# Order of work at four of TensorE's waits: last down block, convolution's way out, expert places, state-space norm

## The chip, the cores and the metric

One core of one Trainium2 chip runs the whole program in one launch. The metric is the device time of an execution in microseconds; shorter is better. All arithmetic is on float32 data. Most matrix products split both operands into a high part (rounded to the matmul's own fp32r format) and a low part (the rest), and add three products: high by high, high by low, low by high.

## The reference, cut to what matters

Two blocks follow each other on a sequence of 256 tokens with 1024 features. The first has two layers, the second two more:

```python
for layer in range(2):                      # first_block
    x = x + 0.5 * rmsnorm(swiglu(rmsnorm(x), gate, up, down))
    hdn = nsa_ssd_mixer(rmsnorm(x), ...) if layer == 0 else rwkv7_time_mix(rmsnorm(x), ...)
    x = x + rmsnorm(hdn)
    x = x + 0.5 * rmsnorm(swiglu(rmsnorm(x), gate, up, down))
for i in range(2):                          # second_block
    mod = silu(c) @ ada_w[i] + ada_b[i]     # shift, scale, gate, shift, scale, gate
    h = rmsnorm(x) * (1 + sc1) + sh1
    y = short_conv_mixer(h) if i == 0 else gated_deltanet_mixer(h)
    x = x + gt1 * rmsnorm(y)
    h = rmsnorm(x) * (1 + sc2) + sh2
    x = x + gt2 * rmsnorm(hier_moe(h))      # 64 experts, each token goes to two; one shared expert
```

The short convolution mixer is `W_out(B * conv3(C * (W x)))`. The mixer with attention and state space puts 512 features of attention and 1024 of the state-space part side by side, the latter gated and normalized in two groups, and multiplies the 1536 by one output matrix. `swiglu` has 2816 hidden features.

## The kernel before, in words

The program is a list of ten stages: Ffn, NsaSsd, Ffn, Ffn, Rwkv, Ffn, Conv, Moe, Delta, Moe. Every engine has its own instruction stream, written out by hand stage by stage in methods `pe`, `act`, `dve`, `pool` and in `sync_program`, and an engine runs its stream strictly in order. The order between engines is kept by named signals: `up` raises one with an instruction, `ge` is waited for. Nothing is planned at run time, so the place of a line in these methods is the order of work.

Weights come in slots of 1 MB. SyncE issues one transfer for each slot, in the order of use, into a ring of six places (more in some stages). A place is free when its last reader has signalled, and SyncE waits for that in order, too. Of a slot, half (128 x 1024) is a unit: ScalarE copies it to the high part (`split_act`, L764, in `Ffn` L922 and L937), VectorE subtracts to get the low part (`split_dve`, L770, in `Ffn` L929 and L943), and TensorE multiplies (`mm3`, L811 to L813). The split parts lie in a buffer of three units, so the split of unit u waits until TensorE has done unit u-3. The data operand is split in the same way in pieces of 128 features, called chunks below: `source_hi` and `source_act` on ScalarE (L783, L793), `source_lo` and `source_dve` on VectorE (L801). Output products (`out_rows_pe`) go through the chunks, and each takes four groups of three matmuls of 512 columns, one group for each of the PSUM banks 0 to 3.

The end of every stage (`back_act`, `back_dve`) squares and sums the four banks on ScalarE as they are done (`y_done`, L694), bank by bank; for each half of the tokens (two banks) it forms the inverse deviation (L697, L710), and VectorE scales (L716) and adds to `x` (L723). The next stage begins with transposes of `x`, which wait for this.

The four places that the change touches:

- **Ffn, last block.** A block b of 256 hidden features has gate and up products, SiLU and product (L976, L1019), a transpose of the result (`turn_pe`, L1085), its split (high part on ScalarE, L981; low part on VectorE, L1025) and the down product (`down_pe`), which adds 24 matmuls to banks 0 to 3. In other blocks the next block's gate and up products lie between the transpose and the down product; behind the last block (b = 10) there is nothing. `down_pe` waits for the low part of the hidden features before its first matmul. VectorE's order in block 10 is: low part of the down weights' second half (L943), then low part of the hidden features (L1025). The last block's loop has the bank outside, so that a bank is done after 6, 12, 18 and 24 matmuls.
- **Conv, way out.** Units 0 to 23 are the input products, two each of the parts B, C and x for four groups of 256 features; units 24 to 31 are the output product. VectorE (L1193 to L1200) and GpSimd (L1220) make the convolution's output chunk by chunk beside the input products. All eight chunks are split after unit 23, since they go into the buffer `x_r`, which the input products read; the splits of units 24 and 25 stand behind them in both queues. TensorE has only the spread of the gain (L678) to do meanwhile.
- **Moe, places.** `select_dve(0)` (L1512, L1514: four operations) makes the matrices by which the tokens of the first four experts are gathered (`gather_pe`, L1527). It stands behind `shared_dve(3)`, which waits for the shared expert's last product.
- **NsaSsd, way out.** The attention's four chunks of `mix` are ready before the state-space part begins. That part ends with the gating (L3133), squares (L3097), sums (`sums_pe`, L603), deviation (L609), reciprocal (L614) and scaling (L3138) of two groups of four chunks. Between the gating and the norm VectorE has a step of the modulation (`fill`, L2025) that waits for TensorE's products of the modulation (L1997, L2007). TensorE's fill of group 8 stands ahead of the output product in its queue; ScalarE then copies that group's row (L2016), which the output product waits for, as banks 2 and 3 hold the modulation. Then ScalarE and VectorE split all 12 chunks, and only then unit `out0 + 2`.

The piece of code that orders the way out of NsaSsd in TensorE's stream is

```python
        self.ssd_pe(e)
        self.x_r = self.x_r_out
        e.wait_ge(*k.ge("attention_out", n, TT - 1))
        e.wait_ge(*k.ge("mod_row", 8))
        e.wait_ge(*k.ge("mod_added", 7))
        self.out_rows_pe(e, self.out0, "mix", 12)
```

## Time and profile before

| | |
|---|---|
| time, median of 3 runs | 3057.51 us (3055.89 to 3057.93) |
| the profiled execution's own time | 3057.37 us |
| its span in the profile | 3055.5 us |
| TensorE busy | 2815.4 us (92%) |
| VectorE, ScalarE, GpSimd busy | 1293.3, 1122.6, 161.4 us |
| mean granted clock of TensorE | 0.958 |
| read from HBM | 697.50 MB |

The span is the time from the first to the last recorded instruction; the execution's own time is 1.9 us longer. A busy share is an average over ten stages with different limits, so it tells where to look and not what an edit is worth. The clock is a share of 2.4 GHz: TensorE is granted either all of it or half (1.2 GHz). Rows name an engine, a line of the kernel and the tensors that are written and read; a value in brackets is the engine's idle time ahead of the instruction, and what ended it.

### The profile page before, as it was taken

What the parts mean: (1) busy time and instruction counts of PE and PEld (TensorE: products, weight loads), DVE (VectorE), ACT (ScalarE), POOL (GpSimd) and SP (SyncE); (2) the same over time, 40 slices, a digit from 0 to 9 for tenths busy, and PEclk for the clock granted to TensorE, in tenths of its full rate; (3) what the DMA queues carried; (4) which work ended last, traced back from release to release, by engine and by line L of the source; (5) the groups of instructions that cost most, each with busy time, mean ns of one, the idle gap of its engine ahead of it and who ended that gap; (6) DMA issues with size and microseconds to landing.
All of it is one profiled execution on the core that took longest, in us unless ns stands there. A gap on an engine that the chain in (4) does not pass through costs nothing.

```text
span 3055.5 us, 44024 instructions
## 1 busy us (share of the span) xinstructions
PE 2815.4 (92%) x18364; PEld 2218.1 (73%) x18364; DVE 1293.3 (42%) x2125; ACT 1122.6 (37%) x2008; POOL 161.4 (5%) x146
## 2 busy tenths in 40 slices
PE   8989878999989998799899999999896879999998
PEld 7879657887878888578697666666695856666665
DVE  5556266546557543464454121212484542221212
ACT  5444245435447222254443222222454251222222
POOL 0000000000000222100010000000002400000000
PEclk9989899999989999799999999999897989999999
DMA  8424656436424111065244899999550036999996
GB/s 338 188 97 165 265 239 268 180 137 234 180 111 193 43 56 56 28 229 195 101 165 159 351 415 415 416 414 417 230 185 1 1 124 255 417 415 418 415 417 252
DMA packets 96402, 701.55 MB, mean 230 GB/s; under 512 B 10688, under 2 KB 10816, under 8 KB 11328
## 3 DMA queue, kind: packets, MB, share of 16 engines
q1 hardware_dynamic: 96192, 698.59, 57.6%
q8 instruction: 151, 2.47, 0.3%
q14 instruction: 59, 0.48, 0.0%
HBM read 697.50 MB, written 1.05 MB: 229 GB/s over the span
## 4 chain that ended last, share of the span: by engine, by line
PE 86%; DVE 6%; ACT 4%; issue 2%; DMA 1%; POOL 1%; SPq 0%; DVEq 0%; ACTq 0%
PE bank L1549 14%; PE bank L811 12%; PE bank L813 12%; PE bank L812 12%; PE bank L1609 8%; PE bank L1527 4%; PE bank L1636 4%; PE bank L1887 2%; PE bank L1895 2%; PE bank L1899 2%; DMA weight_ring<-weight_slots 1%; DVE h_sb L716 1%; PE bank L2402 1%; PE bank L1418 1%; PE bank L1421 1%
## 5 line engine op out<-in xcount | busy, mean ns | idle before, releaser
L1549 PE MATMUL bank<-weight_ring,packed_h 128*64 128x256 f32 x2176 | 285.4, 379 | 0.0
L811 PE MATMUL bank<-source_hi_lo,weight_hi_lo 128*128 128x256 f32 x864 | 250.4, 290 | 13.7 <-DVE source_hi_lo L801 11.7
L1549 PE MATMUL bank<-more_slots,packed_h 128*64 128x256 f32 x1920 | 257.0, 379 | 1.5 <-ACT packed_h L1536 1.5
L811 PE MATMUL bank<-gate_up_hi_lo,x_hi_lo 128*128 128x512 f32 x640 | 253.2, 396 | 1.3 <-DVE gate_up_hi_lo L929 1.3
L1549 PEld LDWEIGHTS bank<-weight_ring,packed_h 128*64 128x64 f32 x2176 | 196.6, 137 | 74.0 <-issue 18.1
L813 PE MATMUL bank<-gate_up_hi_lo,x_hi_lo 128*128 128x512 f32 x640 | 249.7, 390 | 0.0
L812 PE MATMUL bank<-gate_up_hi_lo,x_hi_lo 128*128 128x512 f32 x640 | 249.1, 389 | 0.0
L812 PE MATMUL bank<-source_hi_lo,weight_hi_lo 128*128 128x256 f32 x864 | 247.9, 287 | 0.0
L813 PE MATMUL bank<-source_hi_lo,weight_hi_lo 128*128 128x256 f32 x864 | 247.7, 287 | 0.0
L1549 PEld LDWEIGHTS bank<-more_slots,packed_h 128*64 128x64 f32 x1920 | 174.2, 137 | 69.4 <-issue 15.4
L770 DVE TENSOR_TENSOR weight_hi_lo<-weight_ring,weight_hi_lo 128x1024 fp32r<-128x1024 f32 x138 | 168.0, 1221 | 106.3 <-ACT weight_hi_lo L764 106.2
L1565 DVE TENSOR_TENSOR packed_hidden<-packed_silu,bank 128x256 f32<-128x256 f32 x64 | 27.0, 421 | 415.5 <-ACT packed_silu L1558 415.5
L1626 DVE SCALAR_TENSOR_TENSOR expert_out_hi_lo<-bank,place_gates,expert_out_hi_lo 128x512 fp32r<-128x512 f32 x128 | 96.1, 751 | 223.7 <-ACT expert_out_hi_lo L1620 223.7
L811 PEld LDWEIGHTS bank<-source_hi_lo,weight_hi_lo 128*128 128x128 f32 x864 | 169.4, 196 | 16.7 <-issue 16.1
L943 DVE TENSOR_TENSOR down_hi_lo<-weight_ring,down_hi_lo 128x1024 fp32r<-128x1024 f32 x72 | 87.8, 1224 | 205.5 <-ACT down_hi_lo L937 205.5
L764 ACT ACTIVATE weight_hi_lo<-weight_ring 128x1024 fp32r<-128x1024 f32 x144 | 151.3, 1054 | 61.4 <-PE bank L813 56.8
L1558 ACT ACTIVATE packed_silu<-bank 128x256 f32<-128x256 f32 x64 | 24.6, 384 | 403.9 <-PE bank L1549 403.9
L812 PEld LDWEIGHTS bank<-source_hi_lo,weight_hi_lo 128*128 128x128 f32 x864 | 169.5, 196 | 0.2
L813 PEld LDWEIGHTS bank<-source_hi_lo,weight_hi_lo 128*128 128x128 f32 x864 | 169.4, 196 | 0.0
L937 ACT ACTIVATE down_hi_lo<-weight_ring 128x1024 fp32r<-128x1024 f32 x72 | 75.9, 1059 | 222.0 <-PE bank L813 222.0
L929 DVE TENSOR_TENSOR gate_up_hi_lo<-weight_ring,gate_up_hi_lo 128x1024 fp32r<-128x1024 f32 x128 | 151.5, 1219 | 11.5 <-ACT gate_up_hi_lo L922 11.5
L1609 PE MATMUL bank<-weight_ring,hidden_T 128*64 128x512 f32 x544 | 146.0, 597 | 10.4 <-issue 10.4
(540 smaller groups left out, 5446.7 us busy)
## 6 DMA issues: line engine op xcount, KB each, us to landing
weight_ring<-weight_slots SPq DMA_DIRECT2D x443, 1024.0 KB, 7.6
more_slots<-weight_slots SPq DMA_DIRECT2D x212, 1024.0 KB, 9.0
params_sb<-small_params SPq DMA_DIRECT2D x1, 3196.5 KB, 17.6
h_sb<-weight_slots SPq DMA_DIRECT2D x3, 1024.0 KB, 5.6
y_sb<-weight_slots SPq DMA_DIRECT2D x3, 1024.0 KB, 7.7
x_sb<-x_by_tokens SPq DMA_DIRECT2D x1, 1024.0 KB, 4.9
out_by_tokens<-x_sb SPq DMA_DIRECT2D x4, 256.0 KB, 2.2
params_sb<-small_params SPq DMA_DIRECT2D x1, 69.5 KB, 4.6
```

Of the source, the lines that this page charges most:

```text
L764: e.activation(self.shaped(w[:, 0, :], src), src, ACT.Copy).then_inc(*k.up("weights_hi", self.n, u))
L770: e.tensor_tensor(self.shaped(w[:, 1, :], src), src, self.shaped(w[:, 0, :], src).bitcast(F32), ALU.subtract).then_inc(*k.up(*self.lo_key(u)))
L811: e.matmul(out, w[0], x[0], start=start, stop=False, skip_group_check=shared)
L812: e.matmul(out, w[0], x[1], start=False, stop=False, skip_group_check=shared)
L813: return e.matmul(out, w[1], x[0], start=False, stop=stop, skip_group_check=shared)
L929: e.tensor_tensor(lo, src, hi.bitcast(F32), ALU.subtract).then_inc(*k.up(*self.lo_key("gate_up", j, m)))
L943: e.tensor_tensor(lo, src, hi.bitcast(F32), ALU.subtract).then_inc(*k.up(*self.lo_key("down", b, fc)))
L1527: mm = e.matmul(ps[:, j * T:(j + 1) * T], self.h_tok[:, part, q, c * P:(c + 1) * P], self.sel[g % 2][:, q, :, :].rearrange("p e s -> p (e ...
L1549: mm = e.matmul(ps[x * CAP:(x + 1) * CAP, m * FB:(m + 1) * FB], self.hc[:, c, (2 * (p % 2) + x) * CAP:(2 * (p % 2) + x + 1) * CAP], wt[:, ...
L1609: mm = e.matmul(ps[x * CAP:(x + 1) * CAP, :], self.turned[p % 2][:, fc * P + x * CAP:fc * P + (x + 1) * CAP], wd[:, fc * D + m * 512:fc * ...
L1626: e.scalar_tensor_tensor(out=self.out[p % 2][:, 1, cut], in0=k.banks.at(n, "down", p, m)[:, :], scalar=self.slot_gate[:, p % 2:p % 2 + 1], ...
L1636: mm = e.matmul(k.bank[b][:, :], self.scatter[p % 2][:, b // 2 * P:b // 2 * P + P], self.out[p % 2][:, part, b % 2 * 512:b % 2 * 512 + 512 ...
```

## The change

In `Ffn`, the last block's down product gets a method of its own, `last_down_pe`. It begins with the eight matmuls that need only the high part of the first 128 hidden features, when `hidden_hi` is there, and then does the other sixteen, four for each bank. VectorE makes the low part of the hidden features first and the down weights' low part second. In `Conv`, the chunks of the output get a buffer of their own, `out_hi_lo`; chunks 0 to 5 are split beside the input products (two each at units 8, 14 and 20), and the splits of units 24 and 25 move into the loop. In `Moe`, `select_dve(0)` moves ahead of `shared_dve(3)`. In `NsaSsd`, the attention's four chunks are split during the state-space part, VectorE's step of the modulation moves between the norm's first and second group, and unit `out0 + 2` and the remaining splits alternate with the chunks. No matmul, no transfer and no byte is added or removed.

```diff
@@ -1019,11 +1019,13 @@
                 e.scalar_tensor_tensor(out=self.hid[:, q, :], in0=k.banks.at(n, "gate_up", b, q)[:, FB:2 * FB], scalar=k.x_inv[:, q:q + 1], in1=self.silu[:, q, :],
                                        op0=ALU.mult, op1=ALU.mult).then_inc(*k.up("hidden", n, b, q))
             before, behind = self.around_turn(b)
-            for split in before:
-                self.split_dve(e, split)
+            last = b == FFN_BLOCKS - 1
+            if not last:
+                for split in before:
+                    self.split_dve(e, split)
             e.wait_ge(*k.ge("hidden_hi", n, b))
             e.tensor_tensor(self.hid_r[:, 1, :, :], halves(k.banks.at(n, "hidden_T", b)), self.hid_r[:, 0, :, :].bitcast(F32), ALU.subtract).then_inc(*k.up("hidden_lo", n, b))
-            for split in behind:
+            for split in before if last else behind:
                 self.split_dve(e, split)
         self.back_dve(e, lambda f: self.gain_in(), 0.5)
 
@@ -1087,22 +1089,36 @@
 
     def down_pe(self, e, b):
         k, n = self.k, self.n
-        last = b == FFN_BLOCKS - 1
-        e.wait_ge(*k.ge("hidden_lo", n, b))
 
         def part(bank, fc):
             x, cut = self.hid_r[:, :, fc, bank // 2 * P:bank // 2 * P + P], slice(bank % 2 * 512, bank % 2 * 512 + 512)
-            return self.mm3(e, k.bank[bank][:, :], (x[:, 0, :], x[:, 1, :]), (self.d_r[:, fc, 0, cut], self.d_r[:, fc, 1, cut]), b == 0 and fc == 0, last and fc == 1)
+            return self.mm3(e, k.bank[bank][:, :], (x[:, 0, :], x[:, 1, :]), (self.d_r[:, fc, 0, cut], self.d_r[:, fc, 1, cut]), b == 0 and fc == 0, False)
+        e.wait_ge(*k.ge("hidden_lo", n, b))
         for fc in range(2):
             e.wait_ge(*k.ge(*self.lo_key("down", b, fc)))
-            if not last:
-                for bank in range(4):
-                    mm = part(bank, fc)
-                mm.then_inc(*k.up("down", n, b, fc))
-        if last:
             for bank in range(4):
-                part(bank, 0)
-                part(bank, 1).then_inc(*k.up("y_done", n, bank))
+                mm = part(bank, fc)
+            mm.then_inc(*k.up("down", n, b, fc))
+
+    def last_down_pe(self, e):
+
+        k, n, b = self.k, self.n, FFN_BLOCKS - 1
+
+        def one(bank, fc, part, w_part, stop=False):
+            x, cut = self.hid_r[:, part, fc, bank // 2 * P:bank // 2 * P + P], slice(bank % 2 * 512, bank % 2 * 512 + 512)
+            return e.matmul(k.bank[bank][:, :], x, self.d_r[:, fc, w_part, cut], start=False, stop=stop)
+        e.wait_ge(*k.ge("hidden_hi", n, b))
+        e.wait_ge(*k.ge(*self.lo_key("down", b, 0)))
+        for bank in range(4):
+            one(bank, 0, 0, 0)
+            one(bank, 0, 0, 1)
+        e.wait_ge(*k.ge("hidden_lo", n, b))
+        e.wait_ge(*k.ge(*self.lo_key("down", b, 1)))
+        for bank in range(4):
+            one(bank, 0, 1, 0)
+            one(bank, 1, 0, 0)
+            one(bank, 1, 1, 0)
+            one(bank, 1, 0, 1, True).then_inc(*k.up("y_done", n, bank))
 
     def pe(self, e):
         k, n = self.k, self.n
@@ -1119,7 +1135,7 @@
                 self.gate_up_pe(e, b + 1, 1)
                 if b + 2 < FFN_BLOCKS:
                     self.down_pe(e, b)
-        self.down_pe(e, FFN_BLOCKS - 1)
+        self.last_down_pe(e)
 
 
 class Conv(Stage):
@@ -1133,28 +1149,38 @@
         self.out, self.taps = self.sb("conv_out", [P, C, T]), self.sb("conv_taps", [P, 2, T])
         self.units = []
         self.product_buffers(self.mem)
+        self.x_r_in, self.x_r_out = self.x_r, self.sb("out_hi_lo", [P, 2, C, T], F32R)
         self.plan_units(12, column_half, 2)
         self.plan_units(4, row_half)
 
+    def done_at(self, u):
+
+        return (u // 3 - 2, u // 3 - 1) if u % 6 == 2 and u > 6 else ()
+
     def pe(self, e):
         k, n = self.k, self.n
         self.begin(e)
         self.norm_pe(e)
+        self.x_r = self.x_r_in
         for u in range(24):
             part = u % 6 // 2
             empty = (("conv_b", n, u), ("conv_gate", n, u), ("conv_u", n, u))[part]
             ps = k.banks.take(e, (n, "unit", u), empty)
             self.columns_pe(e, u, ps[:, 0:T], "h" if u == 0 else None)
         self.spread_pe(e, k.gain[:, 0, 1, :])
+        self.x_r = self.x_r_out
         self.out_rows_pe(e, 24, "out")
 
     def act(self, e):
         k, n = self.k, self.n
         e.wait_ge(*k.ge("modulation", 0))
+        self.x_r = self.x_r_in
         self.norm_act(e, k.gain[:, 0, 0, :], k.mod[0][:, 0:C], lambda c: self.source_hi(e, "h", k.h, c, self.h_key(c)), lambda: self.split_act(e, 1))
+        self.x_r = self.x_r_out
         for u in range(24):
-            if u + 2 < 24:
-                self.split_act(e, u + 2)
+            self.split_act(e, u + 2)
+            for c in self.done_at(u):
+                self.source_hi(e, "out", self.out, c, ("conv_out", n, c))
             part, m = u % 6 // 2, u % 2
             c = 2 * (u // 6) + m
             ps = k.banks.at(n, "unit", u)[:, 0:T]
@@ -1167,9 +1193,8 @@
                 e.wait_ge(*k.ge("unit", n, u))
                 e.activation(self.g_T[:, m, :], ps, ACT.Copy).then_inc(*k.up("conv_gate", n, u))
         self.spread_act(e)
-        self.source_act(e, "out", self.out, [("conv_out", n, c) for c in range(C)], ("unit", n, 23))
-        self.split_act(e, 24)
-        self.split_act(e, 25)
+        for c in (6, 7):
+            self.source_hi(e, "out", self.out, c, ("conv_out", n, c))
         for u in range(24, 30):
             self.split_act(e, u + 2)
         self.back_act(e)
@@ -1177,10 +1202,13 @@
     def dve(self, e):
         k, n, K = self.k, self.n, self.TAPS
         e.wait_ge(*k.ge("modulation", 0))
+        self.x_r = self.x_r_in
         self.norm_dve(e, k.gain[:, 0, 0, :], k.mod[0][:, 0:C], lambda c: self.source_lo(e, "h", k.h, c))
+        self.x_r = self.x_r_out
         for u in range(24):
-            if u + 2 < 24:
-                self.split_dve(e, u + 2)
+            self.split_dve(e, u + 2)
+            for c in self.done_at(u):
+                self.source_lo(e, "out", self.out, c)
             part, m = u % 6 // 2, u % 2
             c = 2 * (u // 6) + m
             if part == 2:
@@ -1199,9 +1227,8 @@
                     e.wait_ge(*k.ge("conv_taps", n, c, t - 1))
                     e.scalar_tensor_tensor(out=taps, in0=self.u_T[:, c, t:t + T], scalar=w(t), in1=taps,
                                            op0=ALU.mult, op1=ALU.add).then_inc(*k.up("conv_taps", n, c, t))
-        self.source_dve(e, "out", self.out)
-        self.split_dve(e, 24)
-        self.split_dve(e, 25)
+        for c in (6, 7):
+            self.source_lo(e, "out", self.out, c)
         for u in range(24, 30):
             self.split_dve(e, u + 2)
         self.back_dve(e, lambda f: k.ge("gain_row", n, f))
@@ -1681,7 +1708,6 @@
         return over
 
     def experts_dve(self, e):
-        self.select_dve(e, 0)
         for p in range(self.PAIRS):
             if p == self.PAIRS - 1:
                 over = self.overflow_load(e)
@@ -1833,6 +1859,7 @@
         for u in range(3):
             self.shared_dve(e, u)
         self.ranks_dve(e)
+        self.select_dve(e, 0)
         self.shared_dve(e, 3)
         over = self.experts_dve(e)
         self.overflow_dve(e, over)
@@ -3091,6 +3118,8 @@
         for x, step in self.four_steps():
             k.modulation.fill(e, "ACT", int(step == 2 and x >= 4))
             self.four_act(e, x, step)
+            if step == 2 and x >= 4:
+                self.source_hi(e, "mix", self.mix, x - 4, ("attention_out", n, TT - 1))
         self.sqrt_table(e)
         for c in range(C):
             e.wait_ge(*k.ge("ssd_gated", n, c))
@@ -3131,8 +3160,11 @@
         e.wait_ge(*k.ge("ssd_y", n, 7, 1))
         for c in range(C):
             e.tensor_tensor(self.mix[:, 4 + c, :], self.mix[:, 4 + c, :], self.silu_z[:, c, :], ALU.mult).then_inc(*k.up("ssd_gated", n, c))
-        k.modulation.fill(e, "DVE", 4)
         for g in range(2):
+            for c in (2 * g, 2 * g + 1):
+                self.source_lo(e, "mix", self.mix, c)
+            if g:
+                k.modulation.fill(e, "DVE", 4)
             self.inverse_dve(e, f"ssd{g}", k.rms[:, g, :])
             for c in range(4 * g, 4 * g + 4):
                 e.scalar_tensor_tensor(out=self.mix[:, 4 + c, :], in0=self.mix[:, 4 + c, :], scalar=k.par("ssd_norm")[:, c:c + 1], in1=k.rms[:, g, :],
@@ -3169,11 +3201,15 @@
         e.wait_ge(*k.ge("attended", n, TT - 1, 3))
         self.split_act(e, self.out0)
         self.split_act(e, self.out0 + 1)
+        self.x_r = self.x_r_out
         self.ssd_act(e)
-        self.x_r = self.x_r_out
-        self.source_act(e, "mix", self.mix, [("ssd_out", n, C - 1)] + [None] * 11)
-        for u in range(self.out0, self.out0 + 10):
-            self.split_act(e, u + 2)
+        self.split_act(e, self.out0 + 2)
+        for c in range(C):
+            self.source_hi(e, "mix", self.mix, 4 + c, ("ssd_out", n, c))
+            if c % 2 and c < 6:
+                self.split_act(e, self.out0 + 3 + c // 2)
+        for u in range(self.out0 + 6, self.out0 + 12):
+            self.split_act(e, u)
         self.back_act(e)
 
     def dve(self, e):
@@ -3184,11 +3220,15 @@
         self.attention_dve(e)
         self.split_dve(e, self.out0)
         self.split_dve(e, self.out0 + 1)
+        self.x_r = self.x_r_out
         self.ssd_dve(e)
-        self.x_r = self.x_r_out
-        self.source_dve(e, "mix", self.mix, 12)
-        for u in range(self.out0, self.out0 + 10):
-            self.split_dve(e, u + 2)
+        self.split_dve(e, self.out0 + 2)
+        for c in range(C):
+            self.source_lo(e, "mix", self.mix, 4 + c)
+            if c % 2 and c < 6:
+                self.split_dve(e, self.out0 + 3 + c // 2)
+        for u in range(self.out0 + 6, self.out0 + 12):
+            self.split_dve(e, u)
         self.back_dve(e, lambda f: self.gain_in())
 
     def early_pool(self, e):
```

## Rows read from the trace of the kernel before

**Rows 1.** The page, part 4: shares of the chain that ended last, by engine.

```profile
PE 86%; DVE 6%; ACT 4%; issue 2%; DMA 1%; POOL 1%; SPq 0%; DVEq 0%; ACTq 0%
```

**Rows 2.** TensorE's waits: line, who released it, us in total, times, longest us.

```profile
PE bank L811 <- DVE hidden_hi_lo L1025: 8.4, 4, 2.1
...
PE bank L811 <- DVE weight_hi_lo L770: 7.1, 4, 5.3
...
PE bank L1527 <- issue: 1.6, 2, 0.8
```

**Rows 3.** Timeline of TensorE, last down blocks of Ffn 0 and Ffn 2.

```profile
199.87 0.80 PE L811 MATMUL bank<-down_hi_lo,hidden_hi_lo 128*128 128x512 f32 x1 [2.09 <-DVE hidden_hi_lo L1025]
...
688.20 0.80 PE L811 MATMUL bank<-down_hi_lo,hidden_hi_lo 128*128 128x512 f32 x1 [2.09 <-DVE hidden_hi_lo L1025]
```

**Rows 4.** Timeline of ScalarE, last blocks of Ffn 0 and Ffn 2.

```profile
197.86 0.58 ACT L981 ACTIVATE hidden_hi_lo<-bank 128x512 fp32r<-128x512 f32 x1
...
204.33 0.60 ACT L694 ACTIVATE h_sb<-bank 128x512 f32<-128x512 f32 x1 [0.81 <-PE bank L813]
...
693.72 0.60 ACT L694 ACTIVATE h_sb<-bank 128x512 f32<-128x512 f32 x1 [1.87 <-PE bank L813]
```

**Rows 5.** Timeline of VectorE, last block of Ffn 0.

```profile
197.99 1.22 DVE L943 TENSOR_TENSOR down_hi_lo<-weight_ring,down_hi_lo 128x1024 fp32r<-128x1024 f32 x1 [0.70 <-ACT down_hi_lo L937]
199.13 0.68 DVE L1025 TENSOR_TENSOR hidden_hi_lo<-bank,hidden_hi_lo 128x512 fp32r<-128x512 f32 x1
...
208.11 0.15 DVE L708 TENSOR_SCALAR out_part<-y_square_sums 128x1 f32<-128x1 f32 x1
```

**Rows 6.** Windows: us, busy us of the five engines, granted clock, DMA share, GB/s.

```profile
450.00:452.00 2.00, 0.53 (x3) 0.51 (x4) 1.97 (x7) 1.09 (x5) 0.00 (x0) 1.00 1.00 422
469.30:497.00 27.70, 27.70 (x124) 22.94 (x123) 11.70 (x10) 10.21 (x12) 0.00 (x0) 1.00 0.57 204
1604.98:1609.30 4.32, 4.32 (x10) 3.42 (x11) 2.22 (x2) 0.59 (x1) 0.00 (x0) 0.51 0.42 159
```

**Rows 7.** Timeline of TensorE, way out of Conv.

```profile
1597.70 1.95 PE L678 MATMUL bank<-params_sb,mod_gain 128*128 128x128 f32 x16
1604.98 0.79 PE L811 MATMUL bank<-weight_hi_lo,source_hi_lo 128*128 128x512 f32 x1 [5.34 <-DVE weight_hi_lo L770]
```

**Rows 8.** Timeline of ScalarE, VectorE and GpSimd, Conv.

```profile
1602.63 2.94 ACT L764 ACTIVATE weight_hi_lo<-weight_ring 128x1024 fp32r<-128x1024 f32 x3
...
1582.44 1.22 DVE L770 TENSOR_TENSOR weight_hi_lo<-weight_ring,weight_hi_lo 128x1024 fp32r<-128x1024 f32 x1
1584.88 1.23 DVE L770 TENSOR_TENSOR weight_hi_lo<-weight_ring,weight_hi_lo 128x1024 fp32r<-128x1024 f32 x1 [1.22 <-ACT weight_hi_lo L764]
...
1582.61 1.66 POOL L1220 TENSOR_TENSOR conv_out<-conv_taps,conv_b 128x256 f32<-128x256 f32 x1 [1.27 <-DVE conv_taps L1200]
...
1599.83 0.72 POOL L1220 TENSOR_TENSOR conv_out<-conv_taps,conv_b 128x256 f32<-128x256 f32 x1 [2.14 <-DVE conv_taps L1200]
```

**Rows 9.** Timeline of VectorE, last shared product of Moe 0.

```profile
1678.09 0.42 DVE L1446 TENSOR_TENSOR hid<-silu,bank 128x256 f32<-128x256 f32 x1 [6.70 <-ACT silu L1440]
```

**Rows 10.** The chain in order of time, NsaSsd: start us, us, what.

```profile
448.41 6.85 DMA weight_ring<-weight_slots
```

**Rows 11.** Groups of ScalarE, NsaSsd 410:465: count, busy, mean ns, idle before.

```profile
L3048 ACT ACTIVATE seg_T<-seg_T 128x512 f32<-128x512 f32 x8 | 5.0, 626 | 7.8 <-DVE seg_T L3063 7.8
```

**Rows 12.** Timeline of TensorE, ScalarE, VectorE, way out of NsaSsd.

```profile
456.94 2.80 PE L1997 MATMUL bank<-weight_ring,silu_c 128*32 128x256 f32 x48
465.00 0.77 PE L811 MATMUL bank<-weight_hi_lo,source_hi_lo 128*128 128x512 f32 x1 [5.27 <-DVE source_hi_lo L801]
...
459.86 0.38 ACT L2016 ACTIVATE mod_rows<-bank 128x256 f32<-128x256 f32 x1 [4.18 <-PE bank L1997]
...
457.13 1.74 DVE L614 RECIPROCAL inv_rms<-inv_rms 128x256 f32<-128x256 f32 x1
...
464.43 4.11 DVE L801 TENSOR_TENSOR source_hi_lo<-mix_in,source_hi_lo 128x256 fp32r<-128x256 f32 x12 [0.48 <-ACT source_hi_lo L793]
```

## The prediction

> **What bounds the kernel now.** I read the page first: 86% of the chain that ended last lies on TensorE [rows 1], so an edit is worth what it takes from TensorE's waits, or from the stretches between stages in which TensorE waits for the sums. Next I read TensorE's waits by releaser [rows 2]. The reader is to find in it 8.4 us in four waits for the low part of the hidden features (one in each Ffn), 5.3 us in one wait for weights (Conv; the other three of that row are short), and 1.6 us in two waits ahead of the gather, which the trace puts down to nobody. The fourth place is a wait of 5.3 us for source chunks [rows 12]. Together that is 20.6 us of idle time. The timelines of each place then show what stands in the queue ahead of the releaser [rows 3 to 5, 7 to 9, 12], and windows show the granted clock around them [rows 6]: behind a long wait the matmuls run at the lower level of 1.2 GHz (a mean of 0.51 in Conv) for some four microseconds. So a removed wait can pay twice.
>
> Two speeds recur. At the full clock, 124 matmuls of 512 columns take 27.70 us, 0.223 us each; the first ten in Conv, at a mean clock of 0.51, take 4.32 us, 0.43 us each [rows 6]. Ten matmuls at the full clock would take 2.2 us: a spell of low clock costs 2.1 us.
>
> The sum is made against the profiled execution's own time of 3057.37 us, 0.14 us below the median of the three runs; I subtract from the median at the end.
>
> **Ffn, last block, four times.** The number of matmuls stays at 24. Before, the high part of the hidden features ends at 197.86 + 0.58 = 198.44 [rows 4]; VectorE is at that time in the down weights' low part (197.99, 1.22 us), makes the low part of the hidden features from 199.13 to 199.81, and TensorE begins at 199.87 after 2.09 us of idle time [rows 3, 5]. After, TensorE can begin 0.06 us behind the high part, at 198.5. Its eight matmuls last until 200.3. VectorE takes 0.6 us for the hidden features (the distance to the next instruction is a little less than its length) and 1.22 us for the weights, and is done at 200.3, so that the other sixteen begin at 200.4. The added wait on the second half's low part stands here, and costs under 0.1 us. Behind VectorE's swapped pair nothing is queued but the stage's end.
>
> What counts is not the last bank but the second one: the token half's scaling on VectorE starts with it, and the second half's first operation stands behind it in the queue (208.11 [rows 5]). The second bank is now done with matmul 16, not 12: 200.4 + 8 x 0.223 + 0.3 (its own length, and the longer first one) = 202.5. Before, its square begins at 204.33 [rows 4]. The gain is 1.9 us: the earlier start gives 1.4, the seven or so matmuls that are no longer slow give 7 x 0.21 = 1.4, and four more matmuls ahead of the second bank take 0.9 back. In Ffn 2 the same stretch, first matmul to second square, takes 693.72 - 688.20 = 5.5 us and not 4.5 [rows 3, 4], since the low clock lasts longer; there the gain is 2.9 us. I take 1.9 for the other two: 1.9 + 2.9 + 1.9 + 1.9 = 8.6 us. This holds if the clock stays up. TensorE's wait shrinks from 2.09 to 0.7 us; a wait of 1.7 us in NsaSsd leaves the clock at 1.00, though TensorE is busy for only 0.53 of 2 us [rows 6]. Bounds for one block: at the full clock 1.9 (2.9); at the low level for all sixteen, 16 x 0.43 = 6.9, it would be 1.3 us slower than now; with one spell of 2.1 us, about zero.
>
> **Conv, way out.** Before, the spread of the gain ends at 1597.70 + 1.95 = 1599.65, and TensorE waits 5.34 us for unit 24's low part [rows 7]. In the change units 24 and 25 and chunks 0 to 5 are ready by then: unit 24 may be split once unit 21 is done. So the wait goes whole, 5.3 us, and with it the spell of low clock, 2.1 us: 7.4 us. Late next is unit 26, which needs ScalarE's gain copies and chunks 6 and 7 before it. TensorE needs it after two chunks, 24 x 0.223 = 5.4 us behind 1599.7, at 1605.1. GpSimd's last product ends at 1599.83 + 0.72 = 1600.6 [rows 8]; ScalarE's chunk 0.4 and unit 1.0 (2.94 for three [rows 8]) and VectorE's 1.2 make 1603.3: 1.8 us to spare. The six chunks split in the loop add 0.7 us to VectorE and 0.8 us to ScalarE at three units; VectorE idles 1.22 us ahead of such a unit's split [rows 8], ScalarE still more, since it waits for TensorE there. Without that cover they would cost 0.8 us at each of the three, 2.4 us. The transfers of later slots start earlier with their splits, in the same order.
>
> GpSimd's product of 128x256 took 1.66 us at 1582.61, when VectorE ran the weight split of 1582.44, and 0.72 us at 1599.83, when it ran none [rows 8]. The splits keep their 1.22 us. The Trainium skill, SBUF — State Buffer, section "Who interferes with whom", says that VectorE and GpSimd share one pair of ports under an exclusive lock, and the loser waits; by that, the moved splits could delay chunks 6 and 7. By that rule, with the last two products stretched by 0.9 us each, the part would still be 7.4 us, with nothing to spare; one more such delay would make it 6.5 us. The trace agrees with the rule.
>
> **Moe, places, twice.** VectorE idles 6.70 us ahead of `shared_dve(3)`; the four operations on 128x256, at 0.42 us like the one of the row 1.7 us, fit there [rows 9]. `shared_dve(3)` is not delayed, as they are done before its input is there. TensorE's two waits ahead of the gather go, 1.6 us in both stages together [rows 2]; uncovered, the moved operations could give nothing and cost 1.7 us a stage.
>
> **NsaSsd, way out.** Before, TensorE's last fill product ends at 456.94 + 2.80 = 459.74, and the output product begins at 465.00, after 5.27 us of idle time [rows 12]. After, it waits only for ScalarE's row of group 8, 459.86 + 0.38 = 460.24 [rows 12], and begins at 460.3: 4.7 us. The wait left is 0.6 us, so the low clock goes as well, 2.1 us: 6.8 us. The floor under this is a transfer: group 8's weights land at 448.41 + 6.85 = 455.26 [rows 10] and hold the fill; the change doesn't touch it. Late next is unit `out0 + 2`: the norm's first group began at 457.13, behind the modulation's sum, and ended with the second at 463.9 [rows 12]; freed of that it can begin some 3 us earlier, with four chunks of 0.34 us (4.11 us for twelve) put in. It ends near 461.7, the unit's low part near 463, and TensorE needs it at 460.3 + 5.4 = 465.7. The four chunks that ScalarE copies within the state-space part, 0.4 us each, lie in its idle time, of which 7.8 us stand ahead of the eight operations of L3048 alone [rows 11]; uncovered they would be 1.6 us.
>
> **Sum.** 8.6 + 7.4 + 1.6 + 6.8 = 24.4 us. 3057.5 - 24.4 = 3033.1 us.
>
> **Rivals.** *The clock falls in the last block all the same* (10%). For it: there are two short pauses around the transposes. Against: the 1.7 us wait without a fall. The 8.6 us go, 15.8 stay: 3041.7 us. *A second wait behind the removed one* (7%): unit 26 in Conv or `out0 + 2` in NsaSsd is late, as VectorE has to finish chunks before the split in both. It would take 2 to 3 us each; with half of both starts lost, 5 us: 3038 us. For it: one in-order queue; against: margins of 1.8 and 2.7 us. *The edits do not move the ends* (4%): the next stage is held by transfers that don't start earlier. The DMA share is 0.57 in the NsaSsd product [rows 6], so it would have to be in every stage: 3057 us. *Slower* (3%): the low clock stays through the products that now start without a pause, in Conv and NsaSsd, 96 + 144 matmuls. Each costs 0.21 us more; from 24.4 / 0.21 = 116 such matmuls on the change loses. All 240 would cost 50 us less the 20.2 us of waits gone: 3087 us. Against it: no product in the windows stays low for more than a spell.
>
> **Numbers.** The forecast has 76%. Its own bounds: up to 26.4 us if all Ffn ends give 2.9, with the runs' spread of 1.6 us 3029.5; upwards to the first rival. I take 3029.5 to 3041.8, which leaves out under 2 in 10. About 0.2%, 6 us, can be told from no change by a measurement of this kernel. Faster: 76 + 10 + 7 = 93%; same 4%; slower 3%.
>
> **What would show it.** TensorE's wait on hidden features near 0.7 us and its second square 1.9 us earlier to the start of the block; no wait of L811 on weights in Conv, and L811 behind L678 at the full clock; a wait of 0.6 us on ScalarE's row ahead of the NsaSsd product; no wait ahead of the first gather. A granted clock at the lower level at any of the first three would prove that step wrong, and so would a new wait on L770 at chunk 2.

## Result and profile after

The changed kernel takes 3036.2 us (median of 4 runs, 3035.5 to 3036.9), the kernel before 3057.7 (4 runs, 3055.9 to 3062.0) beside it: a ratio of 0.9928, with a 95% interval of 0.9912 to 0.9944. That is 21.5 us less; 24.4 us had been forecast, 3033.1 us, and the measured time lies within the range. The profiled execution took 3035.50 us over a span of 3033.6 us, 21.9 us below the span of before. What is left to explain is the 2.9 us by which the gain falls short.

The chain of the changed kernel by engine, against [rows 1], has not moved:

```profile
PE 86%; DVE 6%; ACT 4%; issue 2%; DMA 1%; POOL 1%; SPq 0%; DVEq 0%; ACTq 0%
```

TensorE's waits in the changed kernel (line, releaser, total us, times, longest us), against [rows 2]:

```profile
PE bank L1109 <- ACT hidden_hi_lo L981: 2.9, 4, 0.7
PE bank L811 <- DVE weight_hi_lo L770: 2.8, 5, 1.3
```

Four waits of 2.09 us are now four of 0.71 us, on ScalarE. The wait of 5.34 us in Conv is gone. What is left in the row of L770 stands in the Rwkv stage: the 1.3 us (at 962.75) and two of 0.24 us stood there before, two of 0.56 and 0.40 us (at 903.06 and 921.13) are new. The two waits ahead of the gather are not listed any more.

**Ffn 0, last block.** Timelines of TensorE, VectorE and ScalarE, changed kernel, against [rows 3 to 5]:

```profile
198.44 5.83 PE L1109 MATMUL bank<-down_hi_lo,hidden_hi_lo 128*128 128x512 f32 x24 [0.71 <-ACT hidden_hi_lo L981]
...
198.42 0.69 DVE L1027 TENSOR_TENSOR hidden_hi_lo<-bank,hidden_hi_lo 128x512 fp32r<-128x512 f32 x1 [1.19 <-ACT hidden_hi_lo L981]
199.03 1.22 DVE L943 TENSOR_TENSOR down_hi_lo<-weight_ring,down_hi_lo 128x1024 fp32r<-128x1024 f32 x1
...
202.49 0.60 ACT L694 ACTIVATE h_sb<-bank 128x512 f32<-128x512 f32 x1 [0.22 <-PE bank L1109]
...
206.27 0.15 DVE L708 TENSOR_SCALAR out_part<-y_square_sums 128x1 f32<-128x1 f32 x1
```

TensorE starts at 198.44 and does all 24 matmuls without a pause, VectorE is done at 200.25, and the second square comes at 202.49 where it came at 204.33; the second half's first operation follows at 206.27, not 208.11. The start, VectorE's end and the second square were forecast to 0.1 us.

**NsaSsd and Conv, ways out.** Timelines of the changed kernel, NsaSsd first (TensorE, ScalarE, VectorE, then for Conv TensorE, VectorE and GpSimd), against [rows 12] and [rows 7, 8]:

```profile
462.96 0.47 PE L811 MATMUL bank<-weight_hi_lo,source_hi_lo 128*128 128x512 f32 x1 [0.61 <-issue]
...
462.48 0.38 ACT L2043 ACTIVATE mod_rows<-bank 128x256 f32<-128x256 f32 x1 [4.17 <-PE bank L2024]
...
464.20 1.22 DVE L770 TENSOR_TENSOR weight_hi_lo<-weight_ring,weight_hi_lo 128x1024 fp32r<-128x1024 f32 x1
...
1586.11 1.95 PE L678 MATMUL bank<-params_sb,mod_gain 128*128 128x128 f32 x16
1587.81 0.47 PE L811 MATMUL bank<-weight_hi_lo,out_hi_lo 128*128 128x512 f32 x1
...
1590.46 1.23 DVE L770 TENSOR_TENSOR weight_hi_lo<-weight_ring,weight_hi_lo 128x1024 fp32r<-128x1024 f32 x1 [0.53 <-ACT weight_hi_lo L764]
...
1585.37 1.64 POOL L1247 TENSOR_TENSOR conv_out<-conv_taps,conv_b 128x256 f32<-128x256 f32 x1 [12.70 <-DVE conv_taps L1228]
1588.29 0.74 POOL L1247 TENSOR_TENSOR conv_out<-conv_taps,conv_b 128x256 f32<-128x256 f32 x1 [1.28 <-DVE conv_taps L1228]
```

In NsaSsd 0.61 us of the 5.27 us are left, and the first matmul takes 0.47 us and not 0.77. The trace names no releaser for this wait; ScalarE's row ends at 462.86, 0.1 us ahead of the product. In Conv the product follows the spread without a pause; unit 26 is ready at 1591.7 where TensorE reaches it at 1593.4, 1.7 us to spare. Of GpSimd's last two products the first is stretched: 1.64 us beside VectorE's weight split of 1585.21, where it took 0.73 us in the kernel before. The last one takes 0.74 us, with VectorE idle from 1588.2 to 1589.0. So of the two delays that the prediction allowed by the rule of the Trainium skill (SBUF — State Buffer, "Who interferes with whom") one occurs, and it costs nothing: TensorE has no wait in the product.

**Moe, places.** Timelines of TensorE around the first gather, before and after:

```profile
1677.47 1.95 PE L678 MATMUL bank<-params_sb,mod_gain 128*128 128x128 f32 x16
1680.20 1.07 PE L1527 MATMUL bank<-places,h_tokens_hi_lo 128*128 128x256 f32 x7 [0.78 <-issue]
```
```profile
1659.19 1.95 PE L678 MATMUL bank<-params_sb,mod_gain 128*128 128x128 f32 x16
1660.89 1.19 PE L1554 MATMUL bank<-places,h_tokens_hi_lo 128*128 128x256 f32 x8
```

The gather began 2.73 us behind the start of the spread and now begins 1.70 us behind it: 1.03 us for a wait of 0.78 us. The rest is overlap. Where nothing is waited for, a matmul starts 0.25 us before the recorded end of the one ahead of it, and the idle time does not count that.

**Stretch by stretch.** Windows cut at the same events in each kernel show more than the totals: from the last hidden features of an Ffn to the next stage's first transposes (an "end"), from NsaSsd's start to its last fill product, from there to the output product, and so on. Columns: stretch, us, TensorE busy us (matmuls), granted clock, DMA share, GB/s. The kernel before, first profile; in this order: end of Ffn 0, NsaSsd to its last fill product, to the output product, to the next stage, ends of Ffn 2 and 3, Rwkv, Conv's start (to its first product C * x), Conv's way out:

```profile
196.41:211.26 14.85, 8.30 (x30) 0.83 0.20 71
211.26:456.94 245.68, 212.59 (x2091) 0.91 0.55 215
456.94:465.00 8.06, 2.79 (x49) 0.83 0.83 321
465.00:500.55 35.55, 34.83 (x145) 0.94 0.60 225
...
684.74:697.12 12.38, 9.74 (x30) 0.72 0.24 86
...
881.80:896.83 15.03, 8.49 (x31) 0.85 0.19 70
896.83:1318.94 422.11, 378.64 (x2800) 0.93 0.22 83
...
1518.35:1543.19 24.84, 20.26 (x138) 0.75 0.42 154
...
1597.70:1633.26 35.56, 25.98 (x115) 0.90 0.41 151
```

The same nine stretches of the changed kernel:

```profile
196.36:209.41 13.05, 6.96 (x30) 1.00 0.23 82
209.41:459.55 250.14, 216.64 (x2090) 0.89 0.54 211
459.55:462.96 3.41, 2.80 (x50) 1.00 0.78 327
462.96:496.56 33.60, 32.89 (x144) 1.00 0.74 281
...
680.87:690.40 9.53, 6.95 (x31) 1.00 0.31 110
...
874.93:887.99 13.06, 6.97 (x30) 0.90 0.22 80
887.99:1308.42 420.43, 375.76 (x2800) 0.94 0.22 83
...
1505.94:1531.59 25.65, 21.08 (x138) 0.72 0.41 149
...
1586.11:1614.10 27.99, 23.75 (x115) 0.97 0.53 191
```

The edited places gain 1.8 + 2.85 + 2.0 + 1.9 us (Ffn; the last from 14.99 to 13.05), 4.65 + 1.95 (NsaSsd), 7.6 (Conv) and 1.0 twice (Moe, from the router's product to the first hidden features of the experts, 60.04 to 59.01): 24.8 us between these two profiles. The stretches that the diff does not touch take 2.9 us back: NsaSsd up to the fill 4.5, Conv's start 0.8, the first Moe's start 0.9 (9.58 to 10.46), less 1.7 in Rwkv and 1.4 in Delta (308.40 to 306.98), the others 0.1 less. So in this pair of profiles the missing 2.9 us lie where nothing was changed. The experiments ask why, and whether the parts are what the sum took them for.

### The profile page after: what moved, and what is told of

Same layout as the page of the kernel before. It is cut to its first block, busy times and chain, and to the rows that moved or that the text cites. A ratio compares the mean times of both kernels' runs of the same rounds, so it can differ in the third digit from the quotient of the medians.

```text
span 3033.6 us, 44027 instructions
## 1 busy us (share of the span) xinstructions
PE 2805.1 (92%) x18364; PEld 2211.1 (73%) x18364; DVE 1293.2 (43%) x2125; ACT 1121.9 (37%) x2008; POOL 162.3 (5%) x146
## 4 chain that ended last, share of the span: by engine, by line
PE 86%; DVE 6%; ACT 4%; issue 2%; DMA 1%; POOL 1%; SPq 0%; DVEq 0%; ACTq 0%
PE bank L1576 15%; PE bank L811 11%; PE bank L813 11%; PE bank L812 11%; PE bank L1636 8%; PE bank L1554 4%; PE bank L1663 4%; PE bank L1914 2%; PE bank L1922 2%; PE bank L1926 2%; DMA weight_ring<-weight_slots 1%; DVE h_sb L716 1%; PE bank L2429 1%; PE bank L1445 1%; PE bank L1448 1%
## 5 line engine op out<-in xcount | busy, mean ns | idle before, releaser
L770 DVE TENSOR_TENSOR weight_hi_lo<-weight_ring,weight_hi_lo 128x1024 fp32r<-128x1024 f32 x138 | 168.2, 1221 | 100.6 <-ACT weight_hi_lo L764 100.6
```

The source lines that it names most:

```text
L770: e.tensor_tensor(self.shaped(w[:, 1, :], src), src, self.shaped(w[:, 0, :], src).bitcast(F32), ALU.subtract).then_inc(*k.up(*self.lo_key(u)))
```

## Experiments

Medians go with the runs of the kernel before on the same chip. The local times, read from each profile as above, follow the verdicts in one table.

**One part at a time.** Each kernel is the kernel before with one part of the diff, word for word: the last block of the Ffn stages, Conv, Moe, NsaSsd.

> The kernel before with the last block of the four Ffn stages as in the change, and nothing else. Theory (the whole change fell short of the sum because the earlier end of Ffn 0 is taken back in NsaSsd, where TensorE's granted clock falls in other places; the code there is untouched): the four ends still gain 1.85 + 2.75 + 1.9 + 1.8 = 8.3 us by the trace of the changed kernel, NsaSsd takes some 4.3 us back, net about 4 us: 3053.5 us, 0.9987 of before, with a stretch of low clock of over 3 us near 281 and one longer than before from 325. Rival (the parts are worth what the prediction said, and the shortfall comes from the NsaSsd part or from an interplay): 8.3 to 8.6 us faster, 3049 us, 0.9972, the clock between 280 and 345 as before.

> The kernel before with Conv's way out as in the change, and nothing else. All theories: 7.4 us (the wait of 5.3 us and the low clock behind it) less up to 1.3 us for a new short wait of the output product on a weight split, 0.9 us more if the stage behind it gives some back: 3049.5 to 3051.5 us, 0.9974 to 0.9980. It is here as a part of the sum: if NsaSsd, which comes earlier, is unmoved, the clock between 280 and 345 stays as before.

> The kernel before with the places of the first pair made ahead of the shared expert's last quarter in both Moe stages, and nothing else. Prediction's term: 1.6 us, 3056.1 us, 0.9995. By the trace of the changed kernel 1.0 us in the first Moe stage and 1.3 us in the second lie around it, 2.3 us, 0.9992. Rival (nothing on the path): 1.000.

> The kernel before with NsaSsd's way out as in the change, and nothing else. Theory (the part itself works and the loss in NsaSsd comes from the earlier start, which this kernel does not have): 6.3 to 6.8 us faster, 3051 us, 0.9978 to 0.9979, and between 210 and 440 no event moves by more than 0.3 us. Rival (the part causes the loss of 4.3 us ahead of its own place): 2 to 2.5 us faster, 3055 us, 0.9992, with the low clock near 281.

Against 3061.2 us before: Ffn alone 3050.2 us, 0.9964 (0.9951 to 0.9978); Conv alone 3047.1, 0.9957 (0.9944 to 0.9971); Moe alone 3052.2, 0.9974 (0.9963 to 0.9985); NsaSsd alone 3054.4, 0.9971 (0.9959 to 0.9983). Ffn gained 11.0 us by the medians, Conv 14.1, Moe 9.0 and NsaSsd 6.8. NsaSsd alone is what was expected of it; the others gained more than any expectation allowed. The medians add up to 41 us, twice the whole. In the places themselves the parts gain about what was forecast (the table below). The fourth kernel fells the theory on NsaSsd: its Ffn 0 ends as before, yet NsaSsd up to the last fill product takes 7.4 us longer than in the first profile of before:

```profile
211.46:464.56 253.10, 219.18 (x2091) 0.88 0.54 208
```

The low clock near 281 that the Ffn kernel was to show is there (280.4 to 283.8), but so it is in this one (282.5 to 285.9). It could still come from these two parts themselves, so the kernel before and the changed one were run again as they are.

**The same two kernels once more, and the change without its Ffn part.** The third kernel is the changed one with the last block's order of the kernel before.

> The kernel before, unchanged, a second time with a profile. The four kernels with one part each moved by up to 8 us in stretches of NsaSsd (280 to 460) that their code leaves as it was. Theory (the places of TensorE's low clock differ from execution to execution of one and the same program, and carry several us): this profile differs from the first one of the kernel before by 3 us or more at some point of NsaSsd, and the granted clock between 280 and 460 is at the lower level in other places. Rival (the clock follows from the program alone, and each edit moves it): the two profiles agree within 0.5 us everywhere.

> The changed kernel, unchanged, a second time with a profile. Theory (the sum of 24.4 us is right place by place, and the shortfall of some 3 us is the clock in untouched stretches): in this profile the gains between two events on either side of each edited place are again 1.8, 2.7, 1.9, 1.8 (Ffn), 7.5 (Conv), 1 to 1.3 twice (Moe) and 6.4 us (NsaSsd) within 0.4 us, while the whole difference to a profile of before on this chip is anywhere from 18 to 30 us. Rival (NsaSsd always takes 4.3 us back when Ffn 0 ends earlier): the loss of 4 us or more between 210 and 345 against before is there again.

> The changed kernel with the last block of the four Ffn stages as before. Theory (the parts add up, and the clock in untouched stretches only adds spread): 8.4 us slower than the changed kernel on the same chip, within 3 us, some 0.9948 of before. Rival (the earlier end of Ffn 0 costs 4.3 us in NsaSsd each time, which this kernel is spared): 4 us slower than the changed kernel or less, 0.9935 or less of before.

Before 3057.9 us (17 runs, 3052.8 to 3065.4), a second set of the same program 3057.9 (12 runs); changed 3036.9 (6 runs, 3032.8 to 3039.3), 0.9926 (0.9911 to 0.9941): the result again, 20.9 us. Without Ffn 3041.2, 0.9938 (0.9923 to 0.9954): 4.3 us, between the two expectations, and the interval holds both. The second profile of the kernel before, stretches from NsaSsd's start to the fill product and the ends of Ffn 2 and Ffn 3:

```profile
211.49:461.74 250.25, 217.33 (x2090) 0.89 0.54 211
...
689.65:700.88 11.23, 8.20 (x30) 0.85 0.27 95
...
884.71:898.13 13.42, 6.86 (x30) 0.97 0.20 78
```

One program, two executions: NsaSsd differs by 4.6 us at a clock of 0.91 and 0.89 (from 282.9 to 286.3 the second is granted 0.50, the first 1.00), the end of Ffn 3 by 1.6 us at 0.85 and 0.97, with the same wait in it. TensorE's first matmul behind that wait, in the first and in the second profile:

```profile
885.25 0.55 PE L811 MATMUL bank<-down_hi_lo,hidden_hi_lo 128*128 128x512 f32 x1 [2.09 <-DVE hidden_hi_lo L1025]
...
888.16 0.50 PE L811 MATMUL bank<-down_hi_lo,hidden_hi_lo 128*128 128x512 f32 x1 [2.09 <-DVE hidden_hi_lo L1025]
```

In the first the clock falls at 885.6, while the products run; in the second it stays up until 897.3, when they are done. So a wait of this length is followed by low clock in some executions and not in others. The chip is not the reason: 17 executions of the kernel before on one chip took 3052.8 to 3065.4 us, the fastest at a mean granted clock of 0.960, the slowest at 0.954. The Trainium skill (TensorE: Matmul & The Clock Gate, Part 1) says that the phase of the chip's activity monitor runs freely, so that one kernel meets different numbers of slow matmuls from run to run. The page says it of a kernel's start; these profiles show the same in the middle of one. The rival of a fixed loss from Ffn 0's earlier end falls too: without the Ffn part the stretch takes 250.28 us, with it 250.14 and 249.90.

**Three edits of the changed kernel, to test single terms.**

```diff
# e7: last block of Ffn, order of the matmuls
-        for bank in range(4):
+        for bank in range(3):
             one(bank, 0, 0, 0)
             one(bank, 0, 0, 1)
+            if bank < 2:
+                one(bank, 1, 0, 0)
...
# e8: Conv's chunks all behind the loop (the same on ScalarE)
-            for c in self.done_at(u):
-                self.source_lo(e, "out", self.out, c)
...
-        for c in (6, 7):
+        for c in range(C):
             self.source_lo(e, "out", self.out, c)
# e9: NsaSsd, VectorE
+        k.modulation.fill(e, "DVE", 4)
         for g in range(2):
             for c in (2 * g, 2 * g + 1):
                 self.source_lo(e, "mix", self.mix, c)
-            if g:
-                k.modulation.fill(e, "DVE", 4)
```

> The changed kernel with another order in the last block of the Ffn stages: ahead of the wait for the low parts, banks 0 and 1 get three of their six matmuls and bank 2 two, in place of two for each of the four banks; so the second bank is done with matmul 14 and not 16. Theory (the second bank's square sets the end of the stage): from the last hidden features to the next stage's first transposes 12.6 us and not 13.05, 0.45 us (two matmuls) in each of the four ends, 1.8 us in all, too little for the median to show. Rival (the last bank sets it): 13.05 us as before in all four.

> The changed kernel with all eight chunks of Conv's output split after the loop, and only the splits of units 24 and 25 left in it. It tells what the buffer with its early chunks is worth beside the moved weight splits. Theory (after the spread of the gain only chunk 0 is late: ScalarE's copy behind its gain copies, 0.4 us, and VectorE's 0.35 us behind it): TensorE waits 1.4 us for chunk 0 and for nothing else, the clock stays up, and the way out takes 29.4 us from the spread to the next stage and not 27.99. Rival one (the low clock comes with this wait too): 31.5 us. Rival two (unit 26 is late behind eight chunks as well): over 30 us with a second wait on a weight split at the third unit.

> The changed kernel with VectorE's modulation sum ahead of the state-space norm again, as in the kernel before. Theory (the norm then starts 3.1 us later, and the low part of the third unit of the output product, ready at 465.4 in the changed kernel where TensorE reaches it at 468.4, comes 3.8 us later): a wait of 0.8 us at the third unit, and 34.4 us from the product's start to the next stage and not 33.6; the product itself starts as in the changed kernel. Rival (the sum's place is worth the whole wait of before): 3 us or more. Rival two (the margin holds): 33.6 us.

Medians: 3031.6, 3035.1 and 3035.9 us against 3057.9 before, each with an interval of some 6 us either way, which tells none of them from the changed kernel. The stretches tell all three. e7: all four ends take 0.45 us less, as expected. The first, and ScalarE's second square in it:

```profile
197.33:209.93 12.60, 6.96 (x30) 0.95 0.22 84
```
```profile
203.01 0.60 ACT L694 ACTIVATE h_sb<-bank 128x512 f32<-128x512 f32 x1
```

That is 5.05 us behind the turn's first transpose at 197.96, where the changed kernel has 202.49 - 196.99 = 5.50. The second bank sets the end, as the prediction had it. (Conv's start behind the last end takes 25.84 us and not 25.65 to 25.70, which gives part of one of the four back.) e8: TensorE waits once, for a chunk, and the matmul behind it is at the full clock:

```profile
1589.08 0.47 PE L811 MATMUL bank<-weight_hi_lo,out_hi_lo 128*128 128x512 f32 x1 [1.54 <-DVE out_hi_lo L801]
```

The way out takes 29.74 us (29.4 expected), against 27.99 with the early chunks and 35.5 before. So within the way out the moved weight splits are worth 5.8 us and the buffer with its chunks 1.75. The next stage takes part of the buffer's share back: the first Moe's start takes 10.46 us in the changed kernel and 9.60 in e8, so that 0.9 us are left. e9: the product starts as in the changed kernel, 3.40 us behind the fill product, and the third unit is late:

```profile
471.59 0.51 PE L811 MATMUL bank<-weight_hi_lo,source_hi_lo 128*128 128x512 f32 x1 [0.42 <-DVE weight_hi_lo L770]
```

The wait is 0.42 us, not 0.8, but with the overlap of some 0.2 us that it also breaks and a slower matmul behind it the cost is what was expected: from the start of the product to the next stage it is 34.40 us. Of the 6.6 us of this part the sum's place is worth 0.8.

**Work for TensorE while it waits.** In the changed kernel six stages begin with matmuls at the low clock, behind a wait of 4.2 to 7.7 us. The diff is the longer version; the shorter one has 18, 5 and 10 for 34, 8 and 16.

```diff
         for q in range(TT):
+            if q and busy:
+                self.keep_busy(e, busy)
...
     def norm_pe(self, e):
...
+        self.keep_busy(e, 34)
-        self.turn_in_pe(e, self.k.h_tok, lambda q, f: (("scaled_second" if f else "scaled_first", n, q),), lambda c: (self.h_key(c, 0),))
+        self.turn_in_pe(e, self.k.h_tok, lambda q, f: (("scaled_second" if f else "scaled_first", n, q),), lambda c: (self.h_key(c, 0),), 8)
+        self.keep_busy(e, 16)
+
+    def keep_busy(self, e, count):
+        for signal in k.banks.until.get(5, ()):
+            e.wait_ge(*k.ge(*signal))
+        for _ in range(count):
+            e.matmul(k.bank[5][:, 0:P], k.par("ident"), k.par("ident"), start=True, stop=True)
```

> The changed kernel, with extra matmuls of 128 columns on the identity into a free bank where TensorE waits at the start of the six stages that begin with the scaled input (34 ahead of the first transposes, 8 ahead of the second eight, 16 ahead of the first product). Their results are not used. Theory (a wait lets the clock fall, and the low clock behind it is paid by what follows): the clock stays at the full level through these starts; the transposes of the second token half take 1.2 to 1.7 us and not 1.97, and the first product's 3.9 us at the low level take 2 us less; 2 to 3 us for each of six stages, 12 to 18 us faster than the changed kernel, 0.988 of before. Rival (the extra matmuls only bring the low clock elsewhere, or end later than the waits they stand in): the same time or up to 6 us slower.

> The kernel with extra matmuls again, but fewer: 18 ahead of the first transposes, 5 ahead of the second eight, 10 ahead of the first product. In the longer version one extra matmul took 0.225 us at the full clock, so that 34 took 7.65 us in a wait of 5.1 us and each stage began 2.6 us late (15.67 us and not 13.05 for the ends of Ffn); that ate what the clock gave. Theory: 18 fit into the wait (4.05 us of 4.2 to 5.1 us), the ends of Ffn take 13.05 us again, the starts stay at the full clock as in the longer version (Conv's start 21.3 us or less and not 25.7, Rwkv 3 us shorter), and the kernel is 13 to 18 us faster than the changed kernel: 3021 us, 0.988 of before. Rival (in the last microsecond of the wait, which is now empty, the clock falls all the same): the changed kernel's time within 2 us.

The longer one 3039.4 us, 0.9933 (0.9918 to 0.9947); the shorter one 3033.8, 0.9917 (0.9903 to 0.9930). Neither can be told from the changed kernel, where 12 to 18 us had been expected of each. Timeline of TensorE in the shorter one, the end of the last Ffn (extra matmuls, L638) and Conv's start, then its windows for Rwkv, Conv's start and the first Moe's start:

```profile
1504.28 4.29 PE L638 MATMUL bank<-params_sb 128*128 128x128 f32 x36
1509.37 1.07 PE L552 MATMUL bank<-params_sb,y_sb 128*128 128x128 f32 x8 [0.81 <-ACT y_sb L576]
...
1517.84 0.36 PE L822 MATMUL bank<-source_hi_lo,weight_hi_lo 128*128 128x256 f32 x1 [1.81 <-DVE source_hi_lo L812]
```
```profile
891.13:1311.89 420.76, 376.44 (x2831) 0.95 0.22 83
...
1509.37:1532.51 23.14, 20.17 (x168) 1.00 0.47 164
1615.02:1625.24 10.22, 9.00 (x64) 1.00 0.97 407
```

The clock does stay up where TensorE is kept busy: 1.00 in Conv's start, where the changed kernel has 0.72. But the gain is 2.5 us there (25.65 to 23.14), nothing in Rwkv (420.76 us, against 420.43 and 421.03 in the two profiles of the changed kernel) and 0.2 in the first Moe's start (10.46 to 10.22). The second Moe's start takes 10.22 us where the changed kernel has 9.54: its extra matmuls end later than the wait they stand in, and push the first product back. In Conv's start the first product stands at 8.47 us behind the first transposes with or without extra work (25.70 us in the changed kernel's second profile, its first product at 1515.44), since it waits for VectorE's chunk: faster transposes buy nothing, only the product after it. So a low clock costs its full price only where TensorE itself sets the pace. The longer version has 417.70 us in Rwkv, but an end of Ffn 3 of 15.67 us ahead of it, together no less than the changed kernel's 13.06 + 420.43. Why Rwkv gives nothing at 0.95 against 0.94 is open.

Local times by profile, in us. "Ffn ends" are those of Ffn 0, 2, 3 and 5, "Moe places" is the first of the two:

| kernel | median | Ffn ends | NsaSsd to fill | fill to next stage | Conv's start | way out | Moe places |
|---|---|---|---|---|---|---|---|
| before, 1st | 3057.7 | 14.85, 12.38, 15.03, 14.99 | 245.7 | 43.6 | 24.84 | 35.56 | 60.04 |
| before, 2nd | 3057.9 | 15.01, 11.23, 13.42, 14.97 | 250.3 | 43.7 | 24.82 | 35.53 | 60.03 |
| Conv alone | 3047.1 | 15.02, 11.22, 13.45, 14.98 | 246.2 | 43.7 | 24.83 | 27.99 | 60.02 |
| Moe alone | 3052.2 | 14.86, 11.21, 13.44, 14.96 | 245.7 | 43.7 | 24.84 | 35.50 | 59.01 |
| NsaSsd alone | 3054.4 | 15.02, 11.24, 13.42, 14.98 | 253.1 | 37.0 | 24.82 | 35.54 | 60.04 |
| Ffn alone | 3050.2 | 13.06, 9.53, 13.04, 13.07 | 251.8 | 44.4 | 25.68 | 36.05 | 60.03 |
| without Ffn | 3041.2 | 15.02, 11.52, 14.86, 14.97 | 250.3 | 37.0 | 24.81 | 27.99 | 59.01 |
| changed, 1st | 3036.2 | 13.05, 9.53, 13.06, 13.05 | 250.1 | 37.0 | 25.65 | 27.99 | 59.01 |
| changed, 2nd | 3036.9 | 13.06, 9.54, 13.05, 13.05 | 249.9 | 37.0 | 25.70 | 27.99 | 59.01 |

An edited place agrees to 0.05 us between executions once the low clock is out of it; the untouched stretch ahead of NsaSsd's fill spreads over 7.4 us.

Some of what the untouched stretches give and take is steady. With the Ffn edit Conv's start is 0.8 us longer each time, since the low clock that begins behind the Ffn lasts until 14.2 us into the stage and not 12.3, and Rwkv is 0.6 to 2 us shorter (420.4 to 421.1 in the kernels without extra matmuls, against 421.7 to 422.4 without the Ffn edit). The first Moe's start takes 9.6 us in the kernel before, 9.9 with the Conv or the Ffn part alone, and 10.5 with both. Delta, which no edit touches, takes 308.2 to 308.4 us in the kernel before and with NsaSsd alone, but 305.2 with Ffn alone, 305.5 with Conv alone, 306.1 with Moe alone, and 307.0 and 306.8 with the whole change. So three parts each gain 2 to 3 us there by where the low clock falls, and together only 1.4.

What is not settled: the four kernels with one part were faster by 18 us in sum (41 less 22.8) than their places show. By the profiles some 8 us of this lie in Delta, where the parts do not add up. The rest is open. No profile of the kernel before was taken on that chip, where it ran at 3061.2 us; its mean granted clock in the twelve runs there, 0.957, is within 0.0005 of that on the two other chips, which makes some 1 us.

## Why the prediction was right

- **What bounds the kernel, and the method.** Right: every wait that was named shrank as the timelines said, and the chain stayed on TensorE. The whole came out 2.9 us (3.5 us in the second pair of medians) short of the sum, by two terms and by what the sum left out.
- **Ffn, 8.6 us.** Between the first two profiles 8.6 us. Over all profiles of the table without this part, the means are 14.96, 11.47, 13.94 and 14.98 us, against 13.06, 9.53, 13.05 and 13.06 with it: 1.90 + 1.94 + 0.89 + 1.92 = 6.65 us. The mis-sized step is "there the gain is 2.9 us" for Ffn 2 and "1.9 for the other two" for Ffn 3: both took the low clock of one profiled execution for a part of the program. That the first pair of profiles gives the forecast 8.6 us again confirms nothing: it holds the same execution of the kernel before from which the term was read. Where no low clock follows the wait, the end of Ffn 3 gains 0.4 us (13.42 to 13.05), which the terms without the clock, 1.4 less 0.9, had at 0.5. The added wait on the second half's low part cost nothing: the 24 matmuls have no pause.
- **Conv, 7.4 us.** Measured 7.5 in the way out; the first Moe's start takes 0.3 us back with this part alone and 0.9 with the Ffn part too. Unit 26's margin of 1.8 us was measured at 1.7.
- **Moe, 1.6 us.** Measured 1.0 twice, 2.0: the term was 0.4 too small. It took the idle time for the cost of the wait and left out the 0.25 us by which matmuls overlap where nothing is waited for.
- **NsaSsd, 6.8 us.** Measured 4.65 + 1.95 = 6.6. The floor by ScalarE's row held (row 462.86, product 462.96); the margin of `out0 + 2` was 3.0 us, where 2.7 had been worked out.
- **The sum.** 24.4 us forecast; the edited places gain 24.8 us by the first two profiles and 6.65 + 7.5 + 2.0 + 6.6 = 22.8 by the means. The sum had no term for what lies between the edits, where the clock's low stretches shift: 2.9 us back in the first pair. This, and the Ffn term, are the difference to 21.5 and 20.9 us. Two figures beside the sum are wrong and changed nothing: the gain if all Ffn ends gave 2.9 us is 24.4 + 3.0 = 27.4 us, not 26.4, which puts the lower bound at 3028.5; and the "20.2 us of waits gone" under *Slower* are the sum less two spells of low clock, while the waits themselves shrank by some 17 us.
- **Rivals.** The clock did not fall in the last block (1.00 in Ffn 0, and full-speed matmuls in every other). No second wait came behind the removed ones in these products; e9 shows how near it was, 0.4 us with the sum moved back. The low clock did not stay through the products (1.00 in NsaSsd, 0.97 in Conv's way out, whose low part is the next stage's approach).

## What to carry to other kernels

Cut the profiles of both kernels at the same events and compare the stretches: a place that was edited repeats to 0.05 us, while the median of the whole moves by several us with the clock's low stretches, so an edit worth 0.45 us can be shown and one worth 7 to 8 us can look like 4 or 11. Look at the stretch behind the place as well: an earlier end can lengthen the next stage's start by up to 0.9 us, each time. Cost a removed wait in two terms, the idle time for certain and the low clock behind it as a chance, and take the second from more than one execution. To the idle time add the overlap that the wait breaks, 0.25 us at the gather. Of two moves made together ask which carries the gain: in Conv the order of two weight splits gave 5.8 us, the new buffer 1.75, of which 0.9 were left behind the next stage's start. The order of e7 is 1.8 us better at its four places than the changed kernel, and its median is the lowest, 3031.6 us (0.9915, 0.9896 to 0.9933), though the whole time does not separate the two.

## What the runs showed of the hardware

- The places of TensorE's low clock differ between executions of one program, by up to 4.6 us in one stage between two profiles of before; the mean granted clock of 17 executions on one chip lies between 0.954 and 0.960.
- A wait of 2.09 us was followed by low clock in the end of Ffn 3 in two of six profiles without the Ffn edit (15.03 and 14.86 us) and not in the other four (13.42 to 13.45).
- A plain matmul of two f32 operands is recorded as two: 18 extra ones stand as x36 and take 4.29 us, 0.24 us each, while the eight transposes of the same shape take 1.07 us, 0.13 us each. This was not reckoned with in the first version, whose 34 extra matmuls overran the wait and made the stage 2.6 us late (15.67 us where 13.05 stood).
- A matmul that waits for nothing starts before the recorded end of the one ahead, by 0.25 us at the gather, so that a wait recorded as 0.78 us costs 1.03 us.
- GpSimd's product of 128x256 takes 1.64 to 1.66 us beside VectorE's weight split and 0.72 to 0.74 us without it; the split keeps its 1.22 us.
- Extra matmuls in the waits raise the mean granted clock from 0.960 to 0.974 without making the kernel faster by itself.
